# Attention with 128 keys per 64 queries, and the two merges inside a chunk as 64x64 products in quarters of the array

## The chip, the cores and the metric

One core of one Trainium2 chip. The metric is device time in microseconds for the whole layer, the median of the runs of a kernel.

## What is computed

One layer of a streaming encoder on x (1, 2048, 1024) in float32: RMSNorm, one input projection, two head groups, output projection and residual, RMSNorm, squared-ReLU MLP and residual. The change touches both head groups. In the reference, cut to what matters:

```python
# group A: gated DeltaNet, 4 heads of 128, chunks of 64 tokens
a = where(strict, einsum('bhncd,bhnsd->bhncs', kb, k) * decay, 0)
lower = a + eye(64)
u = triangular_solve(lower, v * beta)
w = triangular_solve(lower, kb * exp(gc))
# group B: 8 query heads, 2 key heads of 64; own chunk and the one before
s = einsum('bnqhgd,bnkhd->bnhgqk', qc, kb) * d ** -0.5 - slopes * dist
m = maximum(max(s), sink);  p = exp(s - m)
p = p / (sum(p) + exp(sink - m))
o = einsum('bnhgqk,bnkhd->bnqhd', p, vb)
```

A chunk of 64 queries sees 128 keys: its own 64 and the 64 before them.

## The kernel before, in words

The 2048 tokens are worked on in four groups of 512 (`Fori` over GROUPS), a group in four tiles of 128 tokens, a tile being two chunks. For each group the weights come in 96 units of 1024x128; each is split into a high and a low part, and a unit is 24 products of 128x512. Between the input projections (units up to 23) and the output projection (from unit 24) lies the stage that the change is about. In the words below "the stage" runs in the first group from 182 to 261 us.

**The inverse of group A.** For a tile of 128 tokens and a head the matrix 1 + a is inverted from diagonal blocks of 16. Blocks of 16 are merged to 32 (level 0), to 64 (level 1) and to 128 (level 2). Each level is `masked` (TensorE, line 1480), `mask` (VectorE, 1128), `update` (TensorE, 1501), `extend` (VectorE, 1141), and between levels `turn` (TensorE transposes, 1513) and `flip` (ScalarE copy, 669). At levels 0 and 1 `masked` and `update` are one product of 128x128 weights with 64 moving columns per head, four heads per tile; at level 2 they are 64x64 products that all use one and the same quarter of the array. A product in float32 is two passes of TensorE (two MATMUL records), a transpose one.

**The attention.** A pair of heads j (one in partitions 0 to 63, the other in 64 to 127) and a tile make one of 16 steps n. `sc` (1434) multiplies 128 queries with 192 keys, one product for each of the two heads, on the two row halves of the array. VectorE's `scores` (1088) scales, adds the bias with its mask and takes the maximum, ScalarE's `exps` (637) takes the exponentials, VectorE's `softmax` (1105) the denominator, GpSimd's `probabilities` (379) multiplies. `pt` (1449) turns 256 columns per head (192 and 64 of zeros) in two transposes, ScalarE's `pt_copy` (652) copies them, and `ov` (1457) multiplies with the values `vt`, two accumulated products per head, on the two column halves. In TensorE's order `attend(k)` is sc(k), ov(k-3), pt(k-2).

**The order.** It is written out by hand in each engine's program: the levels with an `attend` between them, then a loop over four tiles (`key_states`, `values`, `state_sum`, `tile_out`, `out_mean`) with the rest of them. Each engine works through its own list and waits on semaphores. VectorE's and ScalarE's lists have the same slots. A `nop(nofuse=True)` makes a wait an instruction of its own instead of a part of the next product.

The values are turned once per group (line 1365, four transposes) from `avr`, and ScalarE copies them to `vt` (602).

## Time and profile before

| | us |
|---|---|
| median of 3 runs | 2516.07 |
| the three runs | 2515.8, 2516.07, 2525.27 |
| the profiled execution, its own time | 2525.63 |
| its span, first to last instruction | 2524.1 |
| TensorE busy | 2469.9 |
| VectorE busy | 1448.5 |
| ScalarE busy | 995.8 |
| GpSimd busy | 166.3 |
| mean granted clock of TensorE | 0.994 |

In the profile PE is TensorE, PEld its weight loads, DVE VectorE, ACT ScalarE, POOL GpSimd. A matmul's duration in the rows holds its way through the array, and those of a run overlap; what one costs is the distance between starts. The forms of a product are given as weights (rows*columns) and then the moving operand (partitions x columns).

### The profile page before, as it was taken

The numbers are of one execution on the slowest core, as the hardware profiler recorded it, in microseconds if no ns is written. First come the engines' busy times: TensorE is split into PE (matmuls) and PEld (weight loads), VectorE is DVE, ScalarE is ACT, GpSimd is POOL, SyncE is SP. The second block draws the span as 40 slices with busy tenths as digits, with TensorE's granted clock in tenths as the row PEclk, the third lists the DMA queues.
The fourth block names the chain that finished last, engine by engine and source line by source line (L and its number), as shares of the span: only waits on it lengthen the run. The fifth ranks groups of instructions, "written<-read, shape, count | busy, mean of one in ns | idle before, by whom it ended". The sixth has DMA issues, their size and how long they took to land.

```text
span 2524.1 us, 36114 instructions
## 1 busy us (share of the span) xinstructions
PE 2469.9 (98%) x12318; PEld 2028.5 (80%) x12318; DVE 1448.5 (57%) x2200; ACT 995.8 (39%) x1829; POOL 166.3 (7%) x189
## 2 busy tenths in 40 slices
PE   5999999999999999999999999999999999999998
PEld 4888788888888878888888877888888887788886
DVE  5677563364677656345466765524556676652544
ACT  4467422232455642222345663212234665322232
POOL 0032000000002200000000210000000131000000
PEclk9999999999998999999999999999999999999999
DMA  4210322334321032223332112322332212233242
GB/s 153 93 59 19 109 93 99 98 101 147 105 91 44 21 113 92 100 94 124 123 110 84 51 51 92 99 95 98 137 116 97 76 43 72 89 98 100 92 142 75
DMA packets 63167, 233.09 MB, mean 92 GB/s; under 512 B 7360, under 2 KB 7360, under 8 KB 62400
## 3 DMA queue, kind: packets, MB, share of 16 engines
q1 hardware_dynamic: 55728, 202.64, 24.1%
q0 software_dynamic: 7312, 28.84, 3.2%
q8 instruction: 70, 1.15, 0.2%
q14 instruction: 57, 0.47, 0.1%
HBM read 223.06 MB, written 8.39 MB: 92 GB/s over the span
## 4 chain that ended last, share of the span: by engine, by line
PE 92%; DVE 4%; ACT 2%; issue 1%; DMA 0%; ACTq 0%; DVEq 0%; POOL 0%; POOLq 0%; SPq 0%
PE ps L1311 90%; PE ps L1454 1%; DVE h_l L1250 1%; PE ps L1516 1%; DVE w_l L794 0%; ACT w_h L444 0%; DVE acc L802 0%; DVE ti L1171 0%; DVE ti L1176 0%; DVE state L1159 0%; ACT h_h L690 0%; DMA stage<-w 0%; PE ps L1398 0%; PE ps L1403 0%; DVE cy L860 0%
## 5 line engine op out<-in xcount | busy, mean ns | idle before, releaser
L1311 PE MATMUL ps<-h_h,w_h 128*128 128x512 f32 x2004 | 790.2, 394 | 16.6 <-DVE w_l L794 7.9
L1311 PE MATMUL ps<-h_l,w_h 128*128 128x512 f32 x2004 | 781.8, 390 | 0.0
L1311 PE MATMUL ps<-h_h,w_l 128*128 128x512 f32 x2004 | 781.6, 390 | 0.0
L794 DVE TENSOR_TENSOR w_l<-stage,w_h 128x1024 fp32r<-128x1024 f32 (+1 forms) x385 | 472.4, 1227 | 281.6 <-ACT w_h L444 267.8
L444 ACT CAST w_h<-stage 128x1024 fp32r<-128x1024 f32 (+1 forms) x385 | 399.7, 1038 | 568.2 <-PE ps L1311 559.3
L1311 PEld LDWEIGHTS ps<-h_h,w_h 128*128 128x128 f32 x2004 | 376.9, 188 | 112.4 <-DVE w_l L794 13.3
L1311 PEld LDWEIGHTS ps<-h_h,w_l 128*128 128x128 f32 x2004 | 377.1, 188 | 79.4
L1311 PEld LDWEIGHTS ps<-h_l,w_h 128*128 128x128 f32 x2004 | 377.2, 188 | 77.6 <-issue 1.9
L1311 PE MATMUL ps<-ff_h,w_h 128*128 128x512 f32 x1036 | 404.6, 391 | 0.0
L1311 PE MATMUL ps<-ff_l,w_h 128*128 128x512 f32 x1036 | 403.1, 389 | 0.0
L1311 PE MATMUL ps<-ff_h,w_l 128*128 128x512 f32 x1036 | 403.1, 389 | 0.0
L758 ACT ACTIVATE ff_h<-fb 128x512 f32 (+1 forms) x128 | 81.0, 633 | 487.2 <-DVE fb L1264 487.2
L1311 PEld LDWEIGHTS ps<-ff_l,w_h 128*128 128x128 f32 x1036 | 194.4, 188 | 41.3 <-issue 1.0
L1311 PEld LDWEIGHTS ps<-ff_h,w_h 128*128 128x128 f32 x1036 | 194.5, 188 | 41.2 <-issue 1.0
L1311 PEld LDWEIGHTS ps<-ff_h,w_l 128*128 128x128 f32 x1036 | 194.4, 188 | 40.4
L1264 DVE SCALAR_TENSOR_TENSOR fb<-ps,rt 128x512 f32<-128x512 f32 x128 | 88.5, 692 | 227.8 <-PE ps L1311 226.6
L1283 DVE TENSOR_TENSOR xs<-ps,xs 128x512 f32 (+1 forms) x64 | 44.3, 693 | 187.8 <-PE ps L1311 187.8
L860 DVE SCALAR_TENSOR_TENSOR cy<-raw,prm,cy 128x512 f32<-128x512 f32 x144 | 107.9, 749 | 14.6 <-DVE cy L856 6.3
L1271 DVE TENSOR_TENSOR ff_l<-ff,ff_h 128x512 f32 (+1 forms) x128 | 88.6, 692 | 25.5 <-ACT ff_h L758 15.5
L1268 DVE TENSOR_TENSOR ff<-fb 128x512 f32<-128x512 f32 x128 | 88.6, 692 | 13.3 <-DVE fb L1264 8.5
L368 POOL DMA_DIRECT2D x_next<-x x20 | 10.7, 537 | 1216.7 <-PE ps L1311 1215.1
L494 ACT COPY raw<-ps 128x512 f32<-128x512 f32 x48 | 28.2, 587 | 148.7 <-PE ps L1311 148.7
(185 smaller groups left out, 2103.3 us busy)
## 6 DMA issues: line engine op xcount, KB each, us to landing
stage<-w SPq DMA_DIRECT2D x385, 512.0 KB, 3.3
x_next<-x POOLq DMA_DIRECT2D x20, 512.0 KB, 6.4
out<-xs POOLq DMA_DIRECT2D x32, 256.0 KB, 2.3
xs<-x POOLq DMA_DIRECT2D x8, 512.0 KB, 4.8
xs<-x POOLq DMA_DIRECT2D x4, 1024.0 KB, 5.3
bia<-bias POOLq DMA_DIRECT2D x1, 1536.0 KB, 7.7
cst<-con SPq DMA_DIRECT2D x1, 704.0 KB, 4.5
prm<-par SPq DMA_DIRECT2D x1, 39.5 KB, 1.9
```

What stands on the lines that cost most here:

```text
L444: act.copy(w_h[:, b, 0:k], stage[:, s, 0:k]).then_inc(w_hi.sem, 1)
L494: act.copy(raw[:, s % 2, 3:], ps[:, A0 + s % 2, :]).then_inc(raw_ready.sem, 1)
L758: act.activation(ff_h[:, i * 4 + s, :], fb[:, s % 2], ACT.Square).then_inc(fh_ready.sem, 1)
L794: dve.tensor_tensor(w_l[:, b, 0:k], stage[:, s, 0:k], w_h[:, b, 0:k].bitcast(F32), ALU.subtract).then_inc(w_lo.sem, 1)
L860: dve.scalar_tensor_tensor(out=cy[:, s % 2], in0=raw[:, s % 2, j:j + TOK], scalar=convw(prm, m, j), in1=cy[:, s % 2], op0=ALU.mult, op1=AL ...
L1250: dve.scalar_tensor_tensor(out=h_l[:, k], in0=xs[:, k], scalar=prm[:, C_N2 + k:C_N2 + k + 1], in1=h_h[:, k].bitcast(F32), op0=ALU.mult, op ...
L1264: dve.scalar_tensor_tensor(out=fb[:, s % 2], in0=ps[:, s % 2, :], scalar=0.0, in1=rt[:], op0=ALU.max, op1=ALU.mult).then_inc(fb_ready.sem, 1)
L1268: dve.tensor_tensor(ff[:, s % 2], fb[:, s % 2], fb[:, s % 2], ALU.mult).then_inc(fp_ready.sem, 1)
L1271: dve.tensor_tensor(ff_l[:, i * 4 + s, :], ff[:, s % 2], ff_h[:, i * 4 + s, :].bitcast(F32), ALU.subtract).then_inc(ff_ready.sem, 1)
L1283: dve.tensor_tensor(xs[:, m, :], ps[:, s // 2 % 2, :], xs[:, m, :], ALU.add).then_inc(res.sem, 1)
L1311: return pe.matmul(o, a, b, start=start, stop=stop)
L1454: last = pe.transpose(o[:, e, c], pp[:, n % 2, e, c * P:c * P + P], I)
```

## The change

Attention: per tile and head pair, the two chunks of 64 queries are multiplied with their own 128 keys each. Scores become four products of 64x64 weights and 128 columns, on four quarters of the array (rows by head, columns by chunk). Scores, bias, exponentials and probabilities are 128 wide instead of 192, and the zero columns (`pads`) go. `pt` is one transpose per head. `ov` is one product per head and chunk with all 128 keys, 64 moving columns. For that the values are kept twice, once shifted by 64 tokens (`vt[:, c, t]`): eight transposes instead of four, and `avr` keeps the last chunk of the group before.

Merges: at levels 0 and 1 each chunk's 64x64 part is a product of its own, chunk 0 in the quarter of rows and columns 0 to 63, chunk 1 in 64 to 127, alternating, with 32 moving columns. `mask` handles 128 columns instead of 256, `extend` becomes two instructions of 64 partitions. Level 2 stays.

No-ops that carry the wait stand now before `sc`, `ov` and all `masked` and `update`.

```diff
         aq = sb("aq", [P, PAIRS, TOK])
         state = sb("state", [P, 2, HEADS, P])
-        vt = sb("vt", [P, 1 + TILES, P])
+        vt = sb("vt", [P, 2, TILES, P])
         cst = sb("cst", [P, N_CONST, P])
         kn = sb("kn", [P, HD + TOK])
         row = sb("row", [64, TOK])
-        bia = sb("bia", [P, 2, PAIRS, 2, KEYS])
+        bia = sb("bia", [P, 2, PAIRS, 2, P])
+        avr = sb("avr", [P, HD + TOK])
+        sb("pad2", [P, 64])
...
-            ss = sb("ss", [P, 2, 2, KEYS], F32, s)
-            pp = sb("pp", [P, 2, 2, 256], F32, s)
-            pts = sb("pts", [P, 2, 2, 2, P], F32, s)
+            ss = sb("ss", [P, 2, 2, P], F32, s)
+            pp = sb("pp", [P, 2, 2, P], F32, s)
+            pts = sb("pts", [P, 2, 4, P], F32, s)
...
+        def chunk(e):
+
+            return slice(HD * e, HD * e + HD)
...
-                    nc.gpsimd.tensor_tensor(pp[:, n % 2, :, HD:], pp[:, n % 2, :, HD:],
-                                            att[:, n % 2, RDEN].unsqueeze(2).to_broadcast([P, 2, KEYS]),
+                    nc.gpsimd.tensor_tensor(pp[:, n % 2], pp[:, n % 2],
+                                            att[:, n % 2, RDEN].unsqueeze(2).to_broadcast([P, 2, P]),
                                             ALU.mult).then_inc(A["p_ready"].sem, 1)
...
-                act.copy(avr[:], ps[:, A0 + 1, :]).then_inc(copied.sem, 1)
+                act.copy(avr[:, 0:HD], avr[:, TOK:]).then_inc(vt_ready.sem, 1)
+                act.wait_ge(vt_ready.sem, vt_ready.after(g, 1))
+                act.copy(avr[:, HD:], ps[:, A0 + 1, :]).then_inc(copied.sem, 1)
...
-                act.copy(vt[:, 0], vt[:, TILES]).then_inc(vt_ready.sem, 1)
-                act.wait_ge(vt_ready.sem, vt_ready.after(g, 1))
                 act.wait_ge(vt_sum.sem, vt_sum.after(g, 1))
-                act.copy(vt[:, 1:], heads(OV)).then_inc(vt_ready.sem, 1)
+                act.copy(vt[:].rearrange("p c t k -> p c (t k)"), ps[:, PT:PT + 2, :]).then_inc(vt_ready.sem, 1)
...
-                        act.activation(pp[:, b, e, HD:], ss[:, b, e], ACT.Exp, bias=att[:, b, NMAX][:, e:e + 1],
+                        act.activation(pp[:, b, e], ss[:, b, e], ACT.Exp, bias=att[:, b, NMAX][:, e:e + 1],
...
-                    act.copy(pts[:, n % 2], ps[:, PT, :].rearrange("p (e c k) -> p e c k", e=2, c=2)).then_inc(A["ptc"].sem, 1)
+                    act.copy(pts[:, n % 2, 0:2], ps[:, PT, 0:256].rearrange("p (e k) -> p e k", e=2)).then_inc(A["ptc"].sem, 1)
...
-                dve.memset(pp[:, :, :, 0:HD], 0.0).then_inc(pads.sem, 1)
...
-                    dve.scalar_tensor_tensor(out=ss[:, b], in0=ps[:, SC:SC + 2, 0:KEYS], scalar=HD ** -0.5,
+                    dve.scalar_tensor_tensor(out=ss[:, b], in0=ps[:, SC:SC + 2, 0:P], scalar=HD ** -0.5,
...
-                        m = dve.tensor_tensor(dl[:, t].rearrange("p (h c) -> p h c", h=HEADS),
-                                              ps[:, lev(t), 0:256].rearrange("p (h c) -> p h c", h=HEADS),
-                                              cst_lev(cst, l).unsqueeze(1).to_broadcast([P, HEADS, 64]), ALU.mult)
+                        m = dve.tensor_tensor(dl[:, t, 0:P].rearrange("p (h c) -> p h c", h=HEADS),
+                                              ps[:, lev(t), 0:P].rearrange("p (h c) -> p h c", h=HEADS),
+                                              cst_lev(cst, l).unsqueeze(1).to_broadcast([P, HEADS, HD // 2]), ALU.mult)
...
-                    tc = first_half(flat(ti[:, t]), l)
-                    dve.tensor_tensor(tc, ps[:, lev(t), 256:512].rearrange("p (n b) -> p n b", b=BLOCK << l), tc,
-                                      ALU.add).then_inc(t_ready.sem, 1)
+                    for e in range(2):
+                        r, b = chunk(e), BLOCK << l
+                        tc = ti[r, t, :, r].rearrange("p h (n two b) -> p h n two b", two=2, b=b)[:, :, :, 0, :]
+                        u = ps[r, lev(t), 256:256 + P].rearrange("p (h n b) -> p h n b", h=HEADS, b=b)
+                        last = dve.tensor_tensor(tc, u, tc, ALU.add)
+                    last.then_inc(t_ready.sem, 1)
...
-                for t in range(TILES):
-                    last = pe.transpose(heads(OV)[:, t], avr[:, t * P:t * P + P], I)
+                for c in range(2):
+                    for t in range(TILES):
+                        at = t * P + HD * c
+                        last = pe.transpose(heads(PT + c)[:, t], avr[:, at:at + P], I)
...
-                    for e in range(2):
-                        r = slice(HD * e, HD * e + HD)
-                        last = mm(ps[:, SC + e, 0:KEYS], aq[r, j, t * P:t * P + P], kn[r, t * P:t * P + KEYS])
+                    pe.nop(nofuse=True)
+                    for c in range(2):
+                        at, own = t * P + HD * c, slice(HD * c, HD * c + HD)
+                        for e in range(2):
+                            r = slice(HD * e, HD * e + HD)
+                            last = mm(ps[own, SC + e, 0:P], aq[r, j, at:at + HD], kn[r, at:at + P])
...
-                    o = ps[:, PT, :].rearrange("p (e c k) -> p e c k", e=2, c=2)
                     for e in range(2):
-                        for c in range(2):
-                            last = pe.transpose(o[:, e, c], pp[:, n % 2, e, c * P:c * P + P], I)
+                        last = pe.transpose(heads(PT)[:, e], pp[:, n % 2, e], I)
...
-                    for e in range(2):
-                        r = slice(HD * e, HD * e + HD)
-                        for c in range(2):
-                            last = mm(heads(OV)[r, j], vt[:, t + c, r], pts[:, n % 2, e, c], c == 0, c == 1)
+                    pe.nop(nofuse=True)
+                    for c in range(2):
+                        q = slice(HD * c, HD * c + HD)
+                        for e in range(2):
+                            r = slice(HD * e, HD * e + HD)
+                            last = mm(heads(OV)[r, j, q], vt[:, c, t, r], pts[:, n % 2, e, q])
...
                     o = ps[:, lev(t), 0:256]
+                    pe.nop(nofuse=True)
                     if l < LEVELS - 1:
-                        four(o.rearrange("p (h n b) -> p h n b", h=HEADS, b=BLOCK << l),
-                             lambda o, h: mm(o, at_[:, t, h], first_half(ti[:, t, h], l)), p_y)
+                        for h in range(HEADS):
+                            for e in range(2):
+                                r = chunk(e)
+                                last = mm(o[r, 32 * h:32 * h + 32].rearrange("p (n b) -> p n b", b=BLOCK << l),
+                                          at_[r, t, h, r], first_half(ti[r, t, h, r], l))
+                        last.then_inc(p_y.sem, 1)
                     else:
-                        pe.nop(nofuse=True)
...
+                    pe.nop(nofuse=True)
                     if l < LEVELS - 1:
-                        four(o, lambda o, h: mm(o, xi[:, t, h], dl[:, t, 64 * h:64 * h + 64]), p_u)
+                        for h in range(HEADS):
+                            for e in range(2):
+                                r = chunk(e)
+                                last = mm(ps[r, lev(t), 256 + 32 * h:288 + 32 * h], xi[r, t, h, r], dl[r, t, 32 * h:32 * h + 32])
+                        last.then_inc(p_u.sem, 1)
                     else:
-                        pe.nop(nofuse=True)
...
-        j = i[i % (2 * b) < b]
-        c[:, K_LEV, 64 * l:64 * l + 64] = (i[:, None] // (2 * b) == j[None, :] // (2 * b)) & (i[:, None] % (2 * b) >= b)
+        j, k = i[(i < HD) & (i % (2 * b) < b)], i % HD
+        c[:, K_LEV, 64 * l:64 * l + HD // 2] = (k[:, None] // (2 * b) == j[None, :] // (2 * b)) & (k[:, None] % (2 * b) >= b)
```

How the instructions stand. First TensorE in level 1, the second of two updates and the `attend` behind it, before the change (xi and dl are the update, kn and aq the scores, pts and vt the values, pp the transposes; the shape is that of the output):

```order
L1503 REGISTER_ALU
L1311 MATMUL ps<-dl,xi 128x64 [waits y_ready]
L1311 MATMUL ps<-dl,xi 128x64 x3
L1438 REGISTER_ALU
L1311 MATMUL ps<-kn,aq 128x192 [waits ss_r]
L1311 MATMUL ps<-kn,aq 128x192
L1311 MATMUL ps<-pts,vt 64x128 [waits ptc]
L1311 MATMUL ps<-pts,vt 64x128 x3
L1454 MATMUL ps<-cst,pp 128x128 [waits p_ready]
L1454 MATMUL ps<-cst,pp 128x128 x3
```

The same place with the change:

```order
L1515 REGISTER_ALU
L1314 MATMUL ps<-dl,xi 64x32 [waits y_ready]
L1314 MATMUL ps<-dl,xi 64x32 x7
L1443 REGISTER_ALU
L1314 MATMUL ps<-kn,aq 64x128 [waits ss_r]
L1314 MATMUL ps<-kn,aq 64x128 x3
L1314 MATMUL ps<-pts,vt 64x64 [waits ptc]
L1314 MATMUL ps<-pts,vt 64x64 x3
L1460 MATMUL ps<-cst,pp 128x128 [waits p_ready]
L1460 MATMUL ps<-cst,pp 128x128
```

Nothing changes places; the update has eight products instead of four, the scores four instead of two, the transposes are two instead of four, and the waits are on the same signals.

Then VectorE in level 1, between two slots of scores, before the change (ti is the inverse, p_u TensorE's signal that an update is done):

```order
L1111 RECIPROCAL att<-att 128x2 [waits den_r]
L1145 TENSOR_TENSOR ti<-ps,ti 128x8x32 [waits p_u] x2
L1091 REGISTER_ALU
L1097 SCALAR_TENSOR_TENSOR ss<-ps,bia 128x384 [waits p_sc]
L1100 TENSOR_REDUCE att<-ss 128x2 [waits ss_r]
```

And with it:

```order
L1111 RECIPROCAL att<-att 128x2 [waits den_r]
L1148 TENSOR_TENSOR ti<-ps,ti 64x4x32 [waits p_u]
L1148 TENSOR_TENSOR ti<-ps,ti 64x4x32
L1148 TENSOR_TENSOR ti<-ps,ti 64x4x32 [waits p_u]
L1148 TENSOR_TENSOR ti<-ps,ti 64x4x32
L1091 REGISTER_ALU
L1097 SCALAR_TENSOR_TENSOR ss<-ps,bia 128x256 [waits p_sc]
L1100 TENSOR_REDUCE att<-ss 128x2 [waits ss_r]
```

Each tile's extension is two instructions of half the partitions, in the same place.

## Rows read from the trace of the kernel before

**Rows 1.** The page: engines' busy time; the chain that ended last, by line.
```profile
PE 2469.9 (98%) x12318; PEld 2028.5 (80%) x12318; DVE 1448.5 (57%) x2200; ACT 995.8 (39%) x1829; POOL 166.3 (7%) x189
...
PE ps L1311 90%; PE ps L1454 1%; DVE h_l L1250 1%; PE ps L1516 1%; DVE w_l L794 0%; ACT w_h L444 0%; DVE acc L802 0%; DVE ti L1171 0%; DVE ti L1176 0%; DVE state L1159 0%; ACT h_h L690 0%; DMA stage<-w 0%; PE ps L1398 0%; PE ps L1403 0%; DVE cy L860 0%
```

**Rows 2.** Windows, group 0's stage: length, busy us, clock, DMA share, GB/s.
```profile
182.00:232.00 50.00, 49.68 (x471) 1.00 0.10 33
232.00:262.00 30.00, 28.81 (x206) 1.00 0.14 41
```

**Rows 3.** Chain of waits, 242 to 248 us: start, us, what.
```profile
242.99 1.12 DVE state L1159 x4
...
246.80 0.69 DVE dl L1151
```

**Rows 4.** Timeline of TensorE, group 0: start, us, instruction, weights, moving, count.
```profile
191.44 0.66 PE L1454 MATMUL ps<-cst,pp 128*128 128x128 f32 x4
191.94 1.91 PE L1516 MATMUL ps<-cst,ti 128*128 128x128 f32 x16
...
195.39 3.68 PE L1311 MATMUL ps<-ti,at 128*128 128x64 f32 x32
199.00 0.59 PE L1311 MATMUL ps<-kn,aq 64*128 64x192 f32 x4
199.53 0.66 PE L1311 MATMUL ps<-pts,vt 128*64 128x128 f32 x8
200.12 0.66 PE L1454 MATMUL ps<-cst,pp 128*128 128x128 f32 x4
```

**Rows 5.** TensorE by form in the stage: busy us, mean ns, idle before.
```profile
L1311 PE MATMUL ps<-at,cst 128*128 128x512 f32 x6 | 3.1, 594 | 0.0
...
L1311 PE MATMUL ps<-ti,at 64*64 64x64 f32 x32 | 2.1, 220 | 0.0
```

**Rows 6.** Timeline of TensorE: second turns, the step into level 2, the first output.
```profile
207.50 1.91 PE L1516 MATMUL ps<-cst,ti 128*128 128x128 f32 x16
...
210.46 0.66 PE L1454 MATMUL ps<-cst,pp 128*128 128x128 f32 x4
211.04 2.07 PE L1311 MATMUL ps<-ti,at 64*64 64x64 f32 x32
...
224.53 0.39 PE L1311 MATMUL ps<-qkvz,state 128*128 128x128 f32 x2
```

**Rows 7.** Timeline of ScalarE: the copy of the turned values.
```profile
117.94 0.59 ACT L602 COPY vt<-ps 128x512 f32<-128x512 f32 x1
```

**Rows 8.** Timeline of TensorE: the first norm's sum, behind the projection.
```profile
122.76 1.02 PE L1311 MATMUL ps<-nq,cst 128*128 128x512 f32 x2
```

**Rows 9.** VectorE by form in the stage: busy us, mean ns, idle before, releaser.
```profile
L1097 DVE SCALAR_TENSOR_TENSOR ss<-ps,bia 128x384 f32<-128x384 f32 x16 | 8.9, 555 | 5.9 <-PE ps L1311 5.4
...
L1134 DVE TENSOR_TENSOR dl<-ps,cst 128x256 f32<-128x256 f32 x8 | 3.3, 421 | 1.8 <-PE ps L1311 1.8
```

**Rows 10.** Windows, group 1's stage: length, busy us, clock, DMA share, GB/s.
```profile
803.20:820.30 17.10, 17.10 (x80) 0.50 0.08 27
```

**Rows 11.** Timeline of TensorE: the starts of the four stages, and group 1's fall.
```profile
181.31 0.28 PE L1430 MATMUL ps<-cst 128*128 128x128 f32 x1
182.32 1.97 PE L1311 MATMUL ps<-ti,at 128*128 128x64 f32 x16 [0.74 <-issue]
...
799.50 0.28 PE L1430 MATMUL ps<-cst 128*128 128x128 f32 x1
800.54 1.97 PE L1311 MATMUL ps<-ti,at 128*128 128x64 f32 x16 [0.76 <-issue]
...
802.96 3.47 PE L1311 MATMUL ps<-ti,at 128*128 128x64 f32 x16
...
1425.70 0.28 PE L1430 MATMUL ps<-cst 128*128 128x128 f32 x1
...
2043.62 0.28 PE L1430 MATMUL ps<-cst 128*128 128x128 f32 x1
```

More of the change, by code:

```diff
@@ L46 @@
 HD = 64
-KEYS = 192
 BLOCK = 16
@@ L131, in build @@
             akr = sb("akr", [P, TOK], F32, s)
-            avr = sb("avr", [P, TOK], F32, s)
             rw = sb("rw", [P, 4, TOK], F32, s)
@@ L249, in build @@
         diag_in = flat(xi[:, 0])
-        diag_ti, diag_xi = (pts[:, n].rearrange("p e c k -> p (e c k)") for n in range(2))
-        diag_turned = ss[:].rearrange("p b e k -> p (b e k)")[:, 0:4 * P]
+        diag_ti, diag_xi = (pts[:, n].rearrange("p e k -> p (e k)") for n in range(2))
+        diag_turned = ss[:].rearrange("p b e k -> p (b e k)")
         def blocks(m, b):
@@ L329, in build @@
         alo = signal("alo", TILES)
-        pads = signal("pads", 1)
         res = signal("res", KT + 2 * KT, credit=1)
@@ L640, in exps @@
                     act.wait_ge(A["nmax"].sem, A["nmax"].after(g, n + 1))
-                    if n == 0:
-                        act.wait_ge(pads.sem, pads.after(g, 1))
                     for e in range(2):
-                        act.activation(pp[:, b, e, HD:], ss[:, b, e], ACT.Exp, bias=att[:, b, NMAX][:, e:e + 1],
+                        act.activation(pp[:, b, e], ss[:, b, e], ACT.Exp, bias=att[:, b, NMAX][:, e:e + 1],
                                        accum_out=att[:, b, SUM][:, e:e + 1])
@@ L821, in _ @@
             dve.memset(kn[:], 0.0)
-            dve.memset(vt[:], 0.0)
+            dve.memset(avr[:], 0.0)
             dve.memset(tb[:], 0.0).then_inc(tb_zeroed, 1)
@@ L1687, in cst_lev @@
 def cst_lev(cst, l):
-    return cst[:, K_LEV, 64 * l:64 * l + 64]
+    return cst[:, K_LEV, 64 * l:64 * l + HD // 2]
 def convw(prm, m, j):
@@ L1715, in constants @@
         b = BLOCK << l
-        j = i[i % (2 * b) < b]
-        c[:, K_LEV, 64 * l:64 * l + 64] = (i[:, None] // (2 * b) == j[None, :] // (2 * b)) & (i[:, None] % (2 * b) >= b)
+        j, k = i[(i < HD) & (i % (2 * b) < b)], i % HD
+        c[:, K_LEV, 64 * l:64 * l + HD // 2] = (k[:, None] // (2 * b) == j[None, :] // (2 * b)) & (k[:, None] % (2 * b) >= b)
     for h in range(HEADS):
         c[32 + h, K_SEL + h] = 1.0
-    q, k = i[:, None], np.arange(KEYS)[None, :]
+    q = i[:, None]
+    k = np.arange(P)[None, :] + HD * (q >= HD)
     dist = np.abs(q + HD - k).astype(np.float32)
-    seen = np.where(q < HD, k < 2 * HD, k >= HD)
-    b = np.zeros((P, 2, PAIRS, 2, KEYS), np.float32)
+    b = np.zeros((P, 2, PAIRS, 2, P), np.float32)
     for j in range(PAIRS):
@@ L1726, in constants @@
             slope = np.float32(2.0 ** -(4 * e + j + 1))
-            b[:, 0, j, e] = np.where(seen & (k >= HD), -slope * dist, NEG)
-            b[:, 1, j, e] = np.where(seen, -slope * dist, NEG)
+            b[:, 0, j, e] = np.where(k >= HD, -slope * dist, NEG)
+            b[:, 1, j, e] = -slope * dist
     return c.reshape(P, -1), b.reshape(P, -1)
```

## The prediction

> **What bounds the kernel now.** I read the page first: TensorE is busy for 2469.9 of 2524.1 us, and 90% of the chain that ended last is products of line 1311 [rows 1]. That says "TensorE", but an average does not say it for the stage that the change touches. So the second view is the windows of the first group's stage: from 182 to 232 us TensorE is busy for 49.68 of 50.00 us, from 232 to 262 for 28.81 of 30 [rows 2]. The first stretch is bound by TensorE alone. In the rest the chain leaves it: in the piece around 243 to 247 us it runs through VectorE's new state (1.12 us) and, after the gated output, the residual (0.69) before a product can start [rows 3]. After 254 us the stage ends in such a chain too, and nothing of the change stands in it. So a microsecond saved on TensorE is worth one in the first stretch and only a part of one in the second.
>
> The third view is TensorE's timeline; each kind of work has a price there from one start to the next, which holds gaps and switches. The fourth is the granted clock, for a reason that comes below.
>
> **The change part by part** (one group; there are four).
>
> *Probabilities turned.* Sixteen times, two 128x128 transposes instead of four. Sixteen transposes span 1.91 us [rows 4] and one lasts 0.28 [rows 11], so they start 0.11 us apart. 32 x 0.11 = 3.5 us saved, certain.
>
> *Probabilities times values.* Eight passes of 128 columns take 0.59 us [rows 4]. A pass of 512 columns takes 0.43 us (two of them span 1.02 us and one lasts 0.59, so the second starts 0.43 after the first [rows 5, 8]), so 0.84 ns a column, 0.107 us for 128. Eight in a row would take 0.86; in 0.59 the two column halves must run side by side, in four steps of 0.107 plus some 0.15 us for the first weight load and the change of shape. Now the passes have 64 columns. A pass of 64 columns with 64 weight columns takes 0.060 us (32 of them from first to last start, (2.07 - 0.22) / 31 [rows 5, 6]). Four steps: 0.24 + 0.15 = 0.39, 0.20 saved, 3.2 us in sixteen. Other end: all eight one after another, 0.63, 0.6 us lost. I take 3.2: halves side by side is what the row shows.
>
> *Scores.* Four passes of 192 columns in 0.53 us [rows 4] (the two row halves side by side). Now eight of 128 columns, on four quarters. All four together: two steps of 0.107 + 0.15 = 0.36, 0.17 saved, 2.7 us in sixteen. If only two run together: 0.58, 0.8 us lost. I take 2.7, as the quarters differ from each other as those halves do, but no row shows four.
>
> *The two merges.* Level 0 and 1 need per tile and merge 8 passes with 128x128 weights; four tiles take 3.61 us [rows 4], so sixteen tile-merges 14.4 us. The moving side has 64 columns (53 ns by the above), so it is the weights, not the columns, that cost 0.11 us a pass. Now 16 passes with 64x64 weights and 32 columns, alternately in two opposite quarters: side by side 8 steps of 0.060 = 0.48 us, 7.7 in all, 6.7 saved. One after another: 0.96 us, 15.4 in all, 1.0 lost. I take 6.7, by nearness to the halves above.
>
> The shortest step in a long run of passes is 0.060 us [rows 6]; no row shows whether the quarter, its weights or the issue of instructions sets it. The Trainium skill speaks against this part. TensorEngine Tiling (section "Instruction Overhead") gives each matmul about 60 cycles of overhead and advises against taking a tiling factor from a dimension that is already small. TensorE: Matmul & The Clock Gate (section "Back-to-back issue gap") has about 62 ns per MATMUL where the sequencer's firmware decodes it; by that figure the 256 passes would be estimated at 15.9 us, 1.5 more than now. The 0.060 us neither refutes nor needs it.
>
> *New waits.* 48 more no-ops carry the waits of scores, values and merges. Level 2 has one per tile already and its passes keep 0.060 us across them [rows 6]: 0. Upper end: 0.08 us each, as the step into level 2 takes 0.58 us after the transposes where the step into the turns takes 0.50 [rows 4, 6]; 3.8 us. All later TensorE work is queued behind such a wait, and VectorE's next scores wait for it in turn; I charge 0.5 us a group for those that come late.
>
> *Values turned.* Eight transposes instead of four: +0.44 us, on the path, as they follow products of TensorE directly. ScalarE's copy of them grows to two banks, some 0.4 us, done by about 119 us while TensorE is in a projection until 122.8 us [rows 7, 8]: 0.
>
> *VectorE, ScalarE, GpSimd.* The scores operation and the maximum go from 384 to 256 elements: 0.55 to 0.42 us each (256 elements cost 0.421 [rows 9]); the mask from 0.42 to 0.29; the update of the inverse from one 0.42 to two of 0.29. So VectorE saves 0.27 a slot and 1.1 us on masks and gives back 1.3 us. ScalarE's exponentials and its copy of the turned probabilities and GpSimd's product shrink too, all beside TensorE. The cleared pads vanish from VectorE before the stage; cover: a TensorE projection.
>
> TensorE's sum: 3.5 + 3.2 + 2.7 + 6.7 = 16.1 us; bounds 16.1 and 1.1. What is late next gives some back. In level 0 the four updates end 1.7 us earlier while VectorE's eight updates of the inverse (2.3 us) come behind a softmax: the turns wait, about 1.2 us. In level 1 the masked products wait for ScalarE's four copies, which stand behind the exponentials of slot 2: about 1.0 us. In the last loop, after the first output, TensorE saves 4 x 0.17 + 7 x 0.20 + 6 x 0.22 = 3.4 us, but VectorE is in the chain [rows 3] and saves 4 x 0.27: I let 2.0 arrive, 1.4 back. Net 16.1 - 1.2 - 1.0 - 1.4 - 0.5 - 0.4 = 11.6 us a group, 46.4 in four.
>
> **The clock.** The granted clock in the profile fell to half (1.2 GHz) for 17.1 us in group 1, from 803.2 us on [rows 10]; what came before was an idle gap of 0.76 us, 16 masked passes and a score [rows 11]. Group 0 had almost the same gap, 0.74 us, and its products kept the full pace [rows 4, 11]. The starts of the stages are 618.2, 626.2 and 617.9 us apart [rows 11], so one fall costs 8.1 us. The profiled execution took 2525.63 us (span 2524.1) with that fall; the median of the three runs is 2516.07, one of them 2525.27, so it goes for a run without (2525.6 - 8.1 = 2517.5).
>
> Sum: 2525.6 - 46.4 = **2479 us** if one fall stays, 2471 without one. A measurement of this kernel tells about 0.5% (12.6 us) from no change.
>
> **The rivals.**
> *Short falls in more groups.* The products that follow the gap are thinner still, and the waits for VectorE add gaps. For it: group 1. Against it: the other group shown. With a fall of group 1's length in every group: 2471 + 4 x 8.1 = 2503; in two, 2487.
> *Slower: the clock stays low.* It falls in each group and no dense stretch lifts it until the second turns or the first tile's output. At the low clock 16 masked passes take 3.47 instead of 1.97 us [rows 11]. Up to the second turns (182.3 to 207.5 us [rows 6, 11]) 15.4 of 25.2 us of work would be left, 30.8 at half clock: 5.6 lost, against 4.4 saved later and 0.4 for the values: 1.6 us a group, 2524. Up to the first output (224.5 us [rows 6]) 29.5 of the 42.2 would be left, 59 at half clock, 15.2 us a group with the rest: 2578. I put it at 2550. It decides from about 24 us of low clock per group (11.6 / 8.1 x 17.1). Against it: group 1 recovered in its first turns, which are still there.
> *Opposite quarters do not run side by side,* or issue sets the pace of a pass. Then the merges lose 1.0 instead of saving 6.7 and the give-backs of 2.2 vanish: 11.6 - 7.7 + 2.2 = 6.1 us a group, 2517.5 - 24 = 2493; with the scores serial as well (3.5 more), 2507. The two sections named above would have it so.
> *Other engines take over.* Each slot needs VectorE, ScalarE, VectorE, GpSimd and TensorE in turn, and 48 waits are dearer when late. If half of the 11.6 us goes, 2494.
>
> **How the numbers follow.** Forecast, with no fall or one: 0.46. Short falls in more groups: 0.15, of which 0.10 faster by over 0.5% (below 2503.5). Clock stays low: 0.18, of which 0.02 is within 0.5%. No side by side: 0.13, of which 0.08 faster. Other engines: 0.08, of which 0.05 faster. Faster: 0.46 + 0.10 + 0.08 + 0.05 = 0.69; slower 0.16; same the rest, 0.15. The range starts where TensorE's whole 16.1 us arrive and no clock falls, 2517.5 - 4 x 15.7 = 2455, and reaches to 2530, which leaves out most of the slow case (0.15) and little below.
>
> **What would show it.** Right: the four merge rows of level 1 at about 1.9 us before the next scores instead of 3.6, scores 0.36, values 0.39, transposes 0.37 us; stages some 607 us apart without a fall. Then VectorE and ScalarE as releasers of TensorE in the turns. Wrong: merge rows at 3.8 us (serial), or a clock of 0.5 in stretches longer than 17 us in several groups.

## The result and the profile after

| | before | after |
|---|---|---|
| median of four runs, us | 2520.14 | 2480.57 |
| the four runs | 2515.8, 2516.07, 2524.22, 2525.27 | 2478.96, 2480.5, 2480.63, 2488.63 |
| the profiled execution, its own time | 2525.63 | 2478.96 |
| TensorE busy | 2469.9 | 2409.9 |
| length of the stage without a fall of the clock | 79.78 | 68.36 to 68.66 |

Of the four runs before, two lie some 8 us above the others, the price of one fall of the clock (the profiled execution, which has one, took 2525.63 us). The ratio after to before is 0.9851, with a 95% interval of 0.9832 to 0.987. The forecast was 2479 us.

The page of the profile of the changed kernel: its engines' busy time and the chain that ended last, by engine and by line (for [rows 1]).

```profile
PE 2409.9 (97%) x12974; PEld 1974.1 (80%) x12974; DVE 1430.0 (58%) x2228; ACT 978.0 (39%) x1829; POOL 156.2 (6%) x189
...
PE 88%; DVE 5%; issue 2%; ACT 2%; POOL 1%; DMA 0%; ACTq 0%; DVEq 0%; POOLq 0%; SPq 0%
PE ps L1314 86%; POOL xi L408 1%; DVE h_l L1253 1%; PE ps L1460 1%; ACT w_h L447 1%; DVE w_l L795 1%; DVE acc L803 0%; DVE tmp L1070 0%; POOL pp L384 0%; DVE ti L1174 0%; DVE ti L1179 0%; DVE state L1162 0%; PE ps L1532 0%; ACT h_h L691 0%; DMA stage<-w 0%
```

TensorE has lost 60 us of busy time and the kernel some 40. GpSimd, which had under half a per cent of the chain before, is in it at two lines: its copies of the inverse's blocks (408) and its product of the probabilities (384).

TensorE's timeline after the change, group 0: first the stage's start and the first levels, then the slots that answer to [rows 4, 6], last the end of the stage (the product that waits for the last low part; before, the same product starts at 261.09).

```profile
181.67 0.28 PE L1435 MATMUL ps<-cst 128*128 128x128 f32 x1
182.68 1.03 PE L1314 MATMUL ps<-ti,at 64*64 64x32 f32 x29 [0.74 <-issue]
...
185.78 1.96 PE L1314 MATMUL ps<-dl,xi 64*64 64x32 f32 x61 [0.38 <-issue]
...
190.75 0.45 PE L1314 MATMUL ps<-pts,vt 128*64 128x64 f32 x8
192.79 0.44 PE L1460 MATMUL ps<-cst,pp 128*128 128x128 f32 x2 [1.59 <-POOL pp L384]
193.16 1.99 PE L1314 MATMUL ps<-ti,at 64*64 64x32 f32 x61
...
195.39 0.45 PE L1314 MATMUL ps<-pts,vt 128*64 128x64 f32 x8
...
197.51 0.45 PE L1314 MATMUL ps<-kn,aq 64*64 64x128 f32 x8 [0.25 <-issue]
...
202.44 0.45 PE L1314 MATMUL ps<-kn,aq 64*64 64x128 f32 x8
202.82 0.45 PE L1314 MATMUL ps<-pts,vt 128*64 128x64 f32 x8
203.20 0.44 PE L1460 MATMUL ps<-cst,pp 128*128 128x128 f32 x2
203.56 2.05 PE L1314 MATMUL ps<-ti,at 64*64 64x64 f32 x29
...
250.03 0.50 PE L1314 MATMUL ps<-h_h,w_h 128*128 128x512 f32 x1 [0.21 <-DVE h_l L1184]
```

From start to start: scores 0.38 us (0.53 before), values 0.38 (0.59), transposes 0.36 ahead of a change of shape (0.58). The merges of level 1 begin at 193.16, the values behind them at 195.39; less 0.38 for the scores between, four tiles of a merge take 1.85 us (3.61 before). The stage, from 181.67 to 250.03, is 68.36 us long instead of 79.78: **11.42 us saved a group**, 7.84 of them up to level 2 (21.89 us from the stage's start instead of 29.73) and 3.58 behind it.

Up to level 2 three waits of TensorE are new: 0.38 us ahead of the first updates, 1.59 us ahead of the second turned probabilities (192.79), and a smaller one ahead of the scores at 197.51, of 0.25 us here and of 0.53 and 0.61 in the second and fourth group. For the last the profile names no releaser ("issue"), and no run was made on it; its cause stays open. For the first two, the chain of waits (start, us, what) says what stands behind the 0.38 us, and VectorE's and GpSimd's timelines what stands behind the 1.59.

```profile
179.85 1.92 POOL xi L408
...
184.62 1.07 POOL xi L408
```

```profile
187.29 2.44 DVE L1148 TENSOR_TENSOR ti<-ps,ti 64x128 f32<-64x128 f32 x8
189.76 0.42 DVE L1097 SCALAR_TENSOR_TENSOR ss<-ps,bia 128x256 f32<-128x256 f32 x1
...
190.75 0.15 DVE L1109 TENSOR_TENSOR att<-att 128x2 f32<-128x2 f32 x1
190.94 0.17 DVE L1111 RECIPROCAL att<-att 128x2 f32<-128x2 f32 x1
191.04 1.23 DVE L795 TENSOR_TENSOR w_l<-stage,w_h 128x1024 fp32r<-128x1024 f32 x1
```

```profile
191.18 1.55 POOL L384 TENSOR_TENSOR pp<-pp,att 128x256 f32<-128x256 f32 x1 [3.11 <-DVE att L1111]
193.60 0.61 POOL L384 TENSOR_TENSOR pp<-pp,att 128x256 f32<-128x256 f32 x1 [0.86 <-DVE att L1111]
```

The softmax of step 1 (lines 1109 and 1111) stands in VectorE's list behind eight updates of the inverse and the scores of step 2. So it ends at 191.1, though ScalarE's exponentials of step 1 were done by 188.4. GpSimd's product then takes 1.55 us instead of 0.61: it starts 0.14 us behind the start of a weight split of VectorE and ends after it. So the wait of 1.59 us has two parts. With a product of 0.61 us it would have been some 0.65 (an estimate, 1.59 - 0.94 from these rows); the late softmax accounts for that part, the meeting with the split for the 0.94.

The clock fell once in the profile, in group 2. The windows of that stage (length, TensorE's busy us, clock, DMA share, GB/s), and its start:

```profile
1395.00:1407.00 12.00, 9.28 (x195) 1.00 0.15 46
1407.30:1420.80 13.50, 13.50 (x185) 0.50 0.11 39
1421.00:1430.00 9.00, 9.00 (x142) 1.00 0.01 2
```

```profile
1395.45 0.28 PE L1435 MATMUL ps<-cst 128*128 128x128 f32 x1
```

It began 11.8 us after the stage's start, just behind the wait of 1.58 us which that group has too. In the kernel before it began at 3.7 us, right behind the first merges [rows 10, 11]. This stage is 73.74 us long, so the fall costs 5.1 to 5.4 us. Every run lists its mean granted clock: 0.998 or 0.999 where no group has a fall, 0.996 for this one. The other three runs have 0.994, 0.994 and 0.990, so by this measure the change has more than one fall in most of its runs. What brings them is the last question below.

### The profile page after: what moved, and what is told of

It reads as the page before. It is cut to its first block, busy times and chain, and to the rows that moved or that the text cites. A ratio compares the mean times of both kernels' runs of the same rounds, so it can differ in the third digit from the quotient of the medians.

```text
span 2477.4 us, 37618 instructions
## 1 busy us (share of the span) xinstructions
PE 2409.9 (97%) x12974; PEld 1974.1 (80%) x12974; DVE 1430.0 (58%) x2228; ACT 978.0 (39%) x1829; POOL 156.2 (6%) x189
## 4 chain that ended last, share of the span: by engine, by line
PE 88%; DVE 5%; issue 2%; ACT 2%; POOL 1%; DMA 0%; ACTq 0%; DVEq 0%; POOLq 0%; SPq 0%
PE ps L1314 86%; POOL xi L408 1%; DVE h_l L1253 1%; PE ps L1460 1%; ACT w_h L447 1%; DVE w_l L795 1%; DVE acc L803 0%; DVE tmp L1070 0%; POOL pp L384 0%; DVE ti L1174 0%; DVE ti L1179 0%; DVE state L1162 0%; PE ps L1532 0%; ACT h_h L691 0%; DMA stage<-w 0%
## 5 line engine op out<-in xcount | busy, mean ns | idle before, releaser
L1314 PE MATMUL ps<-h_h,w_h 128*128 128x512 f32 x2004 | 791.1, 395 | 16.1 <-DVE w_l L795 7.9
```

The costliest lines, as they stand in the source:

```text
L1314: return pe.matmul(o, a, b, start=start, stop=stop)
```

## The experiments

Lengths of the stage below are from its first transpose to the product that waits for the last low part, in a group in which the clock stayed at 1.00, where there is one. Within a kernel they repeat within 0.3 us (0.7 in one kernel); the whole time varies by some 3 to 8 us with each fall.

### Half of the change at a time

The attention alone (the merge code of before in `masked`, `update`, `mask`, `extend` and the constants), and the merges alone (the kernel before with those parts of the diff).

> The attention of the change alone; both merges as before. Theory (each part of the change pays by what it takes off TensorE, and the two parts add up but for the wait at the second turned probabilities): transposes 3.5, values 3.2, scores 2.7 a group, less 1.4 given back in the last loop and 0.6 for values turned and waits, so about 7.4 us a group; stages without a fall of the clock some 611 us apart, total about 0.988 of the kernel before. Rival (the merges made it all, the attention only exchanges TensorE time for waits): under 2 us a group, 616 us or more apart, total above 0.996.

> Both merges as 64x64 products in quarters alone; the attention as before. Theory: four tiles of a merge take 1.9 instead of 3.61 us, so 6.9 us less on TensorE a group, of which about 2 to 2.5 come back as waits at the level 0 (VectorE's updates of the inverse and the second softmax): 4.5 us a group, stages some 613.8 us apart, total about 0.993. If the parts add up, the two savings together make the 11.4 us a group of the whole change. Rival (attention made it all): under 1.5 us a group, total above 0.997.

Attention alone: 2502.83 us, ratio 0.9931 (0.9909 to 0.9953). Merges alone: 2508.39 us, ratio 0.9955 (0.9939 to 0.9972). By these ratios the two parts save 0.69 and 0.45%, together 1.14% of the 1.49% that the whole change saves: a quarter is missing. The stages say otherwise. First and last row of a stage without a fall, attention alone:

```profile
1416.31 0.28 PE L1432 MATMUL ps<-cst 128*128 128x128 f32 x1
...
1489.23 0.50 PE L1311 MATMUL ps<-h_h,w_h 128*128 128x512 f32 x1 [0.21 <-DVE h_l L1181]
```

and merges alone:

```profile
799.53 0.28 PE L1437 MATMUL ps<-cst 128*128 128x128 f32 x1
...
874.97 0.50 PE L1318 MATMUL ps<-h_h,w_h 128*128 128x512 f32 x1 [0.21 <-DVE h_l L1188]
```

Both totals miss what was expected of them (0.988 and 0.993). The stages are 72.92 and 75.44 us long: 6.86 and 4.34 us saved, together 11.20 of the 11.42. **The parts add up; what does not add up is the clock.** In the profile of the attention alone three of the four stages have a fall (some 3.6 us after their start), and cost 5.9 us more each; of the merges alone two have one (13 to 14 us after their start). Against 4 x 6.86 = 27 us only 14.5 arrived in the median of the first. The rival of each (one part made it all) is out.

### Do opposite quarters run side by side?

In the first kernel the four heads of one quarter come first, then those of the opposite one:

```diff
-                        for h in range(HEADS):
-                            for e in range(2):
+                        for e in range(2):
+                            for h in range(HEADS):
```

In the second `for e in range(1)` leaves the second chunk's products out, so a merge has half of its passes.

> The change, with the same products of each merge in another order: the four heads of one quarter first, then the four of the opposite one. Theory A (each quarter has its own queue for some passes, so products of opposite quarters overlap even if they do not alternate): four tiles 1.9 to 2.3 us, nothing slower than 2 us a group. Theory B (only neighbours in the order overlap, and the alternation makes it): in runs of eight passes in one quarter each pass costs 0.060 us, so four tiles take up to 3.7 us and the stage loses up to 7 us a group: stages some 613 us apart, total about 11 us or more above the whole change.

> The change, but the merges of levels 0 and 1 leave the second chunk's products out (half of the passes). Theory A (a quarter sets the pace, 0.060 us for each of its passes): the 32 passes of four tiles still take about 1.9 us, the stage keeps its length within 1 us. Theory B (issue sets the pace of 0.029 us a pass, whatever quarter): 32 passes take about 0.95 us, so up to 3.7 us a group less on TensorE, of which at least 1.5 arrive at the end of the stage.

TensorE's timeline at level 1, quarter by quarter (from the masked products to the values behind them):

```profile
1409.29 0.44 PE L1460 MATMUL ps<-cst,pp 128*128 128x128 f32 x2 [1.47 <-POOL pp L384]
1409.65 2.29 PE L1314 MATMUL ps<-ti,at 64*64 64x32 f32 x61
...
1412.30 0.45 PE L1314 MATMUL ps<-pts,vt 128*64 128x64 f32 x8
```

and with half of the passes:

```profile
1407.50 1.99 PE L1314 MATMUL ps<-ti,at 64*64 64x32 f32 x31
...
1409.72 0.45 PE L1314 MATMUL ps<-pts,vt 128*64 128x64 f32 x8
```

Theory A holds in both. 32 passes in one quarter take 1409.72 - 1407.50 - 0.38 = 1.84 us, as long as 64 passes in two (1.85): a pass costs a quarter 0.057 us, and the issue of one costs at most 0.029. With eight passes in a row for one quarter and then eight for the other, four tiles take 2.27 us, 0.42 more and far from 3.7. So passes already issued for one quarter do not keep those of the other from starting. Stages are 69.03 us long quarter by quarter, 0.4 to 0.7 more than in the change, of the 1.7 that TensorE loses. Its median, 2477.01 us (ratio 0.9858, 0.9823 to 0.9893), lies even below the change's, because three of its four runs have a mean clock of 0.997. In its profile that is one fall, 3.5 us after the first stage's start, which costs 2.6 us. The other three stages have the wait ahead of the second turned probabilities too, 1.46 us (1409.29 above), and no fall behind it. With half of the passes: 2474.77 us; the stage keeps its 69.05 to 69.23 us, a short fall included.

### Four transposes again, and the no-ops doubled

```diff
                     for e in range(2):
+                        pe.transpose(heads(PT)[:, 2 + e], pp[:, n % 2, e], I)
                         last = pe.transpose(heads(PT)[:, e], pp[:, n % 2, e], I)
```

The other kernel has each `pe.nop(nofuse=True)` of `sc`, `ov`, `masked` and `update` twice.

> The change, with each turned probability block transposed twice (the extra one to unused columns of the same bank), so four transposes a step again and nothing else as before. Theory (the prediction's certain term, 3.5 us a group): the transposes' rows go from 0.28 back to 0.50 us, +0.22 us sixteen times; 3.0 to 3.5 us more from the stage's start to its end, stages without a fall 610 us apart. Rival (the last loop and the wait for the second turned block absorb much of it): 1.5 to 2.2 us a group.

> The change, with a second no-op behind each no-op of scores, values and merges: 56 more a group. Theory (a no-op costs nothing while TensorE works off what is queued): under 0.4 us a group. Rival (the prediction's upper end, 0.08 us each): 4.5 us a group on TensorE, at least 3 at the end of the stage.

The transposes took 0.50 us (0.59 ahead of a change of shape) again, so TensorE got its 3.5 us back. Yet the stage grew to 69.73 and 69.78 us, by 1.1 to 1.4: less than even the rival said. Group by group, up to level 2 it lost 0.7 to 1.0 us (22.89 us from the start in the second group, where the change has 22.17) for the 1.3 us of six steps, and the wait ahead of the scores at 197.51 is gone; the ten steps behind level 2 put 2.2 us on TensorE and 0.4 on the stage. There TensorE has slack. The total was 2489.02 us, from two runs, with two falls in the profile.

The doubled no-ops: a stage of 68.19 us, 2483.6 us in total from two runs, with three falls in the profile; in the stage they cost nothing.

### Has VectorE become the next bound?

The maximum over the scores is taken twice, in the change and in the kernel before (`pad2` is spare memory):

```diff
+                    dve.tensor_reduce(pad2[:, 2 * n:2 * n + 2], ss[:, b], AX.X, ALU.max)
                     dve.tensor_reduce(att[:, b, MAX], ss[:, b], AX.X, ALU.max).then_inc(A["amax"].sem, 1)
```

> The change, with VectorE's maximum over 256 scores taken twice in each of the sixteen steps (the extra result is written to spare memory and not used): 0.42 to 0.46 us a step, some 7 us of VectorE a group. Theory (VectorE has become next in line, in the first levels and in the last loop): 2.5 to 5 us more a group, and more than the same insertion costs the kernel before. Rival (VectorE is still hidden everywhere but in the last loop): the same as in the kernel before, 1.5 to 3 us.

> The kernel before, with VectorE's maximum over its 384 scores taken twice in each of the sixteen steps (0.55 us a step, some 9 us of VectorE a group). Theory: TensorE covers it in the first stretch, it shows in the last loop alone, 1.5 to 3 us a group. Rival (VectorE was as close behind before): 4 us or more.

Kernel before: stages 81.72 instead of 79.78, +1.94 us; 2530.08 us in total, ratio 1.0044 (1.0026 to 1.0062). In the change with this addition all four stages had a fall. The shortest is 73.88 us with a fall of 10 us, which costs 3.9 in another kernel (below), so about 70.0 without, an estimate: +1.6 (the other three stages, 75.41 to 75.47 us with a longer fall, give +1.0 to +1.9 by the 5.1 to 5.9 us that such a fall costs elsewhere). That fits the rival and not the 2.5 us or more of the theory: 7 us of VectorE work cost about what 9 did before, and VectorE as such is no closer to being the bound. But TensorE's wait for the second turned probabilities grew, and falls came in every group:

```profile
806.26 0.44 PE L1461 MATMUL ps<-cst,pp 128*128 128x128 f32 x2 [1.91 <-POOL pp L384]
```

The total, 2499.8 us, is 19 above the change's, of which by that estimate 4 x 1.6 = 6.4 are work and the rest is clock.

### Taking the waits away

Two versions of the change in which only the order of two lists differs. In the first, VectorE's:

```diff
                 for t in range(TILES):
                     extend(0, t)
-                attend(2)
-                split_lo(g, CONV, U_OUT - CONV)
+                softmax(1)
+                scores(2)
                 attend(3)
...
                 attend(6)
+                split_lo(g, CONV, U_OUT - CONV)
                 attend(7)
```

in the second also ScalarE's:

```diff
-                attend(2)
+                pt_copy(0)
                 for t in range(TILES):
                     flip(0, t)
+                exps(2)
                 attend(3)
```

and in a third also one product of constants in the standstill at the stage's start, `mm(ps[:, PT, :], I, flat(cst[:, 0:4]))` behind the first transpose.

> The change, with VectorE's list alone in another order: softmax of step 1 behind the eight updates of the inverse instead of behind the scores of step 2, and the split of weight unit 24 four slots later. Theory (TensorE's wait of 1.6 us for the second turned probabilities comes from that place in VectorE's list, and the late falls of the clock, 11 to 14 us after the stage's start, follow that wait): the wait goes; the copies of level 0 behind the exponentials of step 2 come next and leave some 0.6 to 1.0 us of the 1.6 a group; stages 67.5 to 68.0 us long; no fall begins 11 to 14 us after a stage's start, so the runs lie 5 us or more lower for that as well: total 0.980 to 0.983 of the kernel before. Rival (the falls follow from the thin products, not from the wait): stages shorter by the same, but falls as often, total 0.9835 to 0.986.

> As the kernel with VectorE's list in another order, and on ScalarE the four copies of level 0 ahead of the exponentials of step 2. Theory: the masked products of level 1 start 0.5 us or more earlier, stages 67.0 to 67.5 us long, no late falls, total 0.979 to 0.982. Rival: the exponentials of step 2, now later, make the third turned probabilities wait as long, and nothing is gained over the version before.

> As the version with both lists changed, and one product of 128x128 weights with 512 columns of constants (two passes, 0.86 us, the result is overwritten) behind the stage's first transpose, where TensorE stands still for 0.74 us. Theory (the early falls, 3.5 to 4 us after the stage's start, follow that gap): no early falls; the stage no longer by more than 0.1 us; the spread of the runs shrinks to under 3 us. Rival (thin products bring them, the gap is not needed): early falls as often as without it.

VectorE's list alone: 2480.74 us, ratio 0.9855 (0.9837 to 0.9874), no better than the change. The second softmax now comes first and the split is out of the way, so GpSimd's product takes 0.61 us again; which of the two did how much was not tried apart. But the standstill did not go, it moved. TensorE's timeline and the windows of that stage (which starts at 792.23):

```profile
802.06 0.44 PE L1461 MATMUL ps<-cst,pp 128*128 128x128 f32 x2
803.70 2.01 PE L1315 MATMUL ps<-ti,at 64*64 64x32 f32 x61 [1.20 <-ACT xi L673]
```

```profile
803.00:806.00 3.00, 2.30 (x74) 1.00 0.00 0
806.30:816.30 10.00, 10.00 (x119) 0.50 0.01 2
```

The turned probabilities no longer wait, but the first masked products of level 1 wait 1.20 us for ScalarE's copies of level 0 (line 673), which stand behind the exponentials of step 2. The stage without a fall is 68.38 us. And 2.6 us behind that wait the clock falls, as before. My expectation that the late falls would go was wrong for this kernel, since I had them follow from one wait and not from any standstill of that length in that place. A stage with this fall has 72.27 us, 3.9 more.

With ScalarE's copies ahead of the exponentials as well, both waits are gone. TensorE's timeline of group 1 (start of the stage, the same place, its end) and the windows of the four stages, of which the first and the last stand here and all have a clock of 1.00:

```profile
786.89 0.28 PE L1437 MATMUL ps<-cst 128*128 128x128 f32 x1
...
795.93 0.45 PE L1316 MATMUL ps<-kn,aq 64*64 64x128 f32 x8 [0.30 <-DVE ss L1098]
...
796.70 0.44 PE L1462 MATMUL ps<-cst,pp 128*128 128x128 f32 x2
797.06 1.99 PE L1316 MATMUL ps<-ti,at 64*64 64x32 f32 x61
...
853.92 0.50 PE L1316 MATMUL ps<-h_h,w_h 128*128 128x512 f32 x1 [0.23 <-DVE h_l L1185]
```

```profile
181.00:250.00 69.00, 64.92 (x843) 1.00 0.14 43
...
1997.00:2066.00 69.00, 64.91 (x843) 1.00 0.14 42
```

**2467.18 us (2465.51 to 2467.64), ratio 0.9791 (0.9774 to 0.9808)**: faster than both kernels, 13 us below the change. The stage is 66.90 to 67.06 us, 1.5 us shorter, which makes 6 of the 13; the clock is 0.998 or 0.999 in all five runs, and the rest comes from that. The third version gave 2467.04 us (ratio 0.9793, 0.9777 to 0.981) and stages of 66.94 to 66.99: the product in the gap costs nothing. Since the version without it had no early falls, whether it would prevent them stays open.

### Standstill or thin work?

The better order took away waits and moved work, so it doesn't say which of the two had brought the falls. The last kernel is the change, with TensorE kept busy in its wait (`mm` is a float32 product, two passes):

```diff
                 def pt(n):
+                    if n == 1:
+                        for i in range(3):
+                            mm(ps[:, PT, 256:512], I, flat(cst[:, 0:2]))
                     pe.wait_ge(A["p_ready"].sem, A["p_ready"].after(g, n + 1))
```

> The change, and ahead of the second turned probabilities, where TensorE waits 1.6 us for GpSimd, three products of constants with 256 columns (six passes, some 1.3 us, the result goes to unused columns and isn't read). The work that follows stays as thin as it was. Theory (the falls 11 to 14 us after the stage's start follow from that standstill): the stage keeps its 68.3 to 68.6 us, and the falls of that place go, in the profile and in the timed runs, so the median comes to 2473 to 2476 us where the change has 2480.6. Rival (the thin products of level 1 bring the falls, whatever stands before them): falls as often as in the change, median 2479 to 2482.

The same place in TensorE's timeline of group 1 (stage's start 788.10), and the four stages' windows:

```profile
797.20 0.45 PE L1314 MATMUL ps<-pts,vt 128*64 128x64 f32 x8
797.58 1.56 PE L1314 MATMUL ps<-cst 128*128 128x256 f32 x6
799.24 0.44 PE L1463 MATMUL ps<-cst,pp 128*128 128x128 f32 x2
799.61 1.99 PE L1314 MATMUL ps<-ti,at 64*64 64x32 f32 x61
```

```profile
181.00:250.00 69.00, 65.09 (x843) 1.00 0.13 41
788.00:857.00 69.00, 64.83 (x842) 1.00 0.12 40
1395.00:1464.00 69.00, 65.11 (x844) 1.00 0.13 40
2002.00:2071.00 69.00, 64.86 (x841) 1.00 0.12 40
```

The turned probabilities start 11.14 us into the stage (11.12 in the change), the stages are 68.22 to 68.90 us long, and what follows is as thin as ever. But there is no fall, in the profile or in the five runs (0.998 or 0.999), and the median is **2472.19 us (2470.65 to 2473.37), ratio 0.9807 (0.9785 to 0.983): 8.4 us less than the change, for six more passes a group whose result nobody reads.** The kernel before, timed with it, had a clock of 0.995 in four of its nine runs, so falls came there too. The theory holds: the late falls need TensorE standing still there.

They do not follow from it every time. In the profiles of all kernels here, 27 stages have a standstill of 1.2 to 1.9 us at this place, and 14 of them a fall that begins 11 to 14 us after the stage's start (1 of 4 in the change, 4 of 4 at 1.91 us, 0 of 3 quarter by quarter at 1.46). Of the 12 stages of the two kernels with both lists changed and of this last one, none has any. The early falls, some 3.5 us after the start, are another matter: the standstill of 0.74 us before them is in every stage but those of the third version, and they came in 1 of 4 stages before the change, in 3 of 4 with the attention alone, in 4 of 4 with half of the passes, and in none of the change's profile. What decides there stays open.

## Why the prediction was right, and where it was not

*The sum on TensorE* was right. Start to start, merges save 4 x (3.61 - 1.85) = 7.0 us a group (6.7 forecast), scores 16 x 0.15 = 2.4 (2.7), values 16 x 0.21 = 3.4 (3.2), transposes 3.5 (3.5): 16.3 against 16.1.

*Quarters side by side* was right. It was taken from the likeness to the halves, and left open what sets the 0.060 us. The runs say it: a quarter needs 0.057 us a pass, whatever the opposite one does, and issue isn't in the way. The scores, for which no row had shown four quarters, take 0.38 us where four together were to take 0.36 and only two together 0.58. Of the two sections of the Trainium skill weighed there, TensorE: Matmul & The Clock Gate (section "Back-to-back issue gap") has about 62 ns per MATMUL where firmware decodes it, and an issue floor of about 25 ns otherwise; here 64 passes took 1.85 us, 0.029 a pass, which rules out the first figure for this case and lies just above the second. The Trainium skill's TensorEngine Tiling (section "Instruction Overhead") advises against tiling a small dimension; here the moving side went from 64 to 32 columns with the tiling, and the time halved, since two quarters work at once.

*Values turned* lie outside of the stage. From one stage's start to the next, less the stage, are 538.41 us before and 538.59 after in the first group, and 538.1 to 538.4 before and 538.2 to 538.8 after in all: some 0.2 more on average, which this spread doesn't tell from the 0.44 forecast. ScalarE's copy of them takes 1.01 us instead of 0.59 and shows nowhere.

*No-ops* were put at 0 with 0.5 for late ones; 0 was right, also at double their number.

*What is given back* was 4.9 us (16.3 - 11.4) where 4.1 was forecast with the no-ops' 0.5. The size was near, the place was not, so that this agreement is in part luck. Forecast was that the turns of level 0 wait for VectorE's updates of the inverse (1.2) and the masked products of level 1 for ScalarE's copies (1.0). The turns waited for nothing. Instead the updates wait 0.38 us for GpSimd's copies of the blocks, and the second turned probabilities 1.59 for a softmax behind those eight updates and a product that met a weight split; 0.25 to 0.6 more are lost ahead of later scores. The queue was the right one, but I had asked only who waits for the updates, not what else stands behind them in VectorE's list, and the 0.94 us of the long product stood in no term. The ScalarE wait was there too, hidden behind the other: it came up at 1.20 us as soon as that was gone. Behind level 2 TensorE saves 8 x 0.15 + 11 x 0.21 + 10 x 0.22 = 5.7 us and 3.6 arrive, so 2.1 are given back, where the last loop was to give back 1.4. VectorE is in the way there, as forecast: TensorE's waits for its residual grew (the longest before was 0.30 us).

```profile
236.91 1.16 PE L1314 MATMUL ps<-dl,xi 128*128 128x128 f32 x8 [0.73 <-DVE dl L1154]
```

The four-transposes kernel shows that the 2.2 us of these 5.7 that the transposes save are worth 0.4 at most. "Certain" was thus true of TensorE's 3.5 us for the transposes, not of the stage, which gets 1.1 to 1.4.

*The clock.* One fall of 8.1 us was in the forecast, taken over from the kernel before. The profiled execution had one of 5.1 to 5.4 us, the other runs lower mean clocks. Without any, the change would be at 2478.96 - 5.2 = 2473.8 us, which the kernel with a busy TensorE confirms (2472.2), against 2471 forecast. So the rival "short falls in more groups" was in part what happened: the median lies 7 us above the time without falls, where the forecast had 8. The median came out 2 us from the forecast with the right total and a partly wrong reason, which is luck in the clock's part. The falls aren't those of the kernel before, behind the first merges, but new ones behind a new wait.

*Other rivals.* The clock did not stay low: in its profile one fall, shorter than 14 us. *Other engines take over*: not as a bound, but the late steps of theirs at one place cost about as much in clock as in waiting (some 7 us in the median against 4 x 1.59).

## What to carry to other kernels

Where TensorE is made faster, ask not only who waits for the longer list of another engine, but which small step stands last in it: here a softmax of 0.3 us, two places too late, and a product of GpSimd that met a weight split of VectorE cost 1.6 us of waiting a group, and as much again in clock. When whole times of parts don't add up, compare lengths of the stage in groups with the clock at 1.00; and when the clock falls, look at what TensorE stood still for in the few microseconds before. Reordering two lists was worth 13 us, a third of what the whole change had brought.

## What the runs showed of the hardware

- Opposite quarters of the array work on passes at the same time, even if eight passes in a row go to one and the next eight to the other (2.27 us against 1.85 alternating, and against 1.84 for one quarter alone).
- A 64x64 pass takes its quarter 0.057 us with 32 columns and 0.060 with 64 [rows 5, 6]: in this range columns set hardly any of it. Eight passes of 64x64 weights and 128 columns on all four quarters take 0.38 us.
- Behind a standstill of 1.2 to 1.9 us in the thin first third of the stage the granted clock fell from 2.4 to 1.2 GHz within 3 us in 14 of 27 stages; with six passes without use in its place it fell in none of five runs, by their mean clocks.
- A fall's price depends on its length and on what lies in it: 8.0 us for 17 us of low clock in the kernel before, 5.1 to 5.4 for some 13.5 in the change, 3.9 for 10 with the other order of VectorE's list, 2.6 for 10 quarter by quarter. With half of the passes left out, a fall began 3.5 us after the start of all four stages, yet the stages stayed within 0.9 us of the change's; that the slower work filled the time in which TensorE waits otherwise is likely, but wasn't tried apart.
- GpSimd's product and VectorE's weight split held each other up, whichever came second. Where the product started just behind the split, in all 32 such stages of eight kernels, 128x256 took 1.55 us in place of 0.61. In the kernel before, the product starts 0.21 us ahead of the split in all four groups; it keeps its 0.83 us, and the split takes 1.69 in place of 1.23. With the split moved away, the product took 0.61 again.
